# The block-doubling inverse of a gated DeltaNet layer on 32 by 32 and 64 by 64 tiles of TensorE's array

## What is computed

```python
a_low = jnp.where(strict, jnp.einsum('bhnid,bhnjd->bhnij', kb, k) * decay, 0.0)
t_mat = a_low + jnp.eye(C, dtype=a_low.dtype)
u = lax.linalg.triangular_solve(t_mat, vb, left_side=True, lower=True, unit_diagonal=True)
w = lax.linalg.triangular_solve(t_mat, kb * jnp.exp(gc)[..., None], left_side=True,
                                lower=True, unit_diagonal=True)
```

## Time and profile before

| | us |
|---|---|
| median of 3 runs (1456.88 to 1458.3) | 1457.95 |
| profiled execution, its own time | 1457.2 |
| span of that execution | 1455.2 |
| TensorE busy | 1433.1 (98%) |
| VectorE busy | 857.0 (59%) |
| ScalarE busy | 546.8 (38%) |
| POOL busy | 110.1 (8%) |

### The profile page before, as it was taken

The page is one execution under the profiler, slowest core; times in us unless marked ns, Lnnn a source line. Parts: engine busy times, 40 slices in busy tenths (PEclk is TensorE's granted clock), DMA queues, the critical chain, the costliest instruction groups (busy, mean ns, idle before and its releaser), DMA issues.

```text
span 1455.2 us, 28065 instructions
## 1 busy us (share of the span) xinstructions
PE 1433.1 (98%) x11980; PEld 1413.1 (97%) x11980; DVE 857.0 (59%) x1428; ACT 546.8 (38%) x1068; POOL 110.1 (8%) x149
## 2 busy tenths in 40 slices
PE   8999999999999999999999999999999999999997
PEld 8999999999999999999989999999999999999997
DVE  7746895778555554332486468958775555543334
ACT  5135563556222222222441364625562222222222
POOL 0001212100000100000000012221000000000000
PEclk9999999999999999999999999999999999999999
DMA  5332342122344333222213313411223433332221
GB/s 195 106 103 73 95 117 73 44 67 100 106 141 138 131 131 131 95 87 91 84 59 103 115 59 95 117 59 59 88 81 119 141 131 131 131 111 93 88 94 67
DMA packets 57692, 147.38 MB, mean 101 GB/s; under 512 B 19041, under 2 KB 22497, under 8 KB 57569
## 3 DMA queue, kind: packets, MB, share of 16 engines
q1 hardware_dynamic: 49744, 119.89, 25.3%
q0 software_dynamic: 7824, 25.70, 5.0%
HBM read 132.78 MB, written 12.78 MB: 100 GB/s over the span
## 4 chain that ended last, share of the span: by engine, by line
PE 89%; DVE 7%; ACT 2%; issue 1%; DMA 1%; SPq 0%; DVEq 0%; ACTq 0%
PE PS L566 73%; PE PS L572 4%; DVE Wl L1601 1%; DVE hT L1639 1%; PE PS L861 1%; PE PS L863 1%; DVE Xl L1618 1%; PE PS L844 1%; DVE mT L1638 1%; PE PS L755 1%; DVE conv L1726 1%; PE PS L1073 1%; PE PS L893 0%; PE PS L739 0%; PE PS L727 0%
## 5 line engine op out<-in xcount | busy, mean ns | idle before, releaser
L566 PE MATMUL PS<-Xh,Wh 128*128 128x260 f32 x2464 | 503.5, 285 | 3.3 <-DVE Xl L1660 2.7
L566 PE MATMUL PS<-Xl,Wh 128*128 128x260 f32 x2464 | 498.0, 283 | 0.0
L566 PE MATMUL PS<-Xh,Wl 128*128 128x260 f32 x2464 | 495.9, 283 | 0.0
L1141 ACT ACTIVATE Wh<-stage 128x1024 fp32r<-128x1024 f32 x211 | 223.6, 1060 | 654.7 <-PE PS L566 647.7
L566 PEld LDWEIGHTS PS<-Xh,Wh 128*128 128x128 f32 x2464 | 382.2, 189 | 6.7 <-DVE Xl L1660 3.1
L566 PEld LDWEIGHTS PS<-Xh,Wl 128*128 128x128 f32 x2464 | 379.9, 188 | 0.0
L566 PEld LDWEIGHTS PS<-Xl,Wh 128*128 128x128 f32 x2464 | 379.7, 189 | 0.0
L1601 DVE TENSOR_TENSOR Wl<-stage,Wh 128x1024 fp32r<-128x1024 f32 x211 | 258.0, 1223 | 183.5 <-ACT Wh L1141 183.0
L566 PE MATMUL PS<-actH,Wh 128*128 128x260 f32 x616 | 124.1, 283 | 0.0
L566 PE MATMUL PS<-actH,Wl 128*128 128x260 f32 x616 | 124.0, 282 | 0.0
L566 PE MATMUL PS<-actL,Wh 128*128 128x260 f32 x616 | 123.7, 282 | 0.0
(11 more groups left out here) (324 smaller groups left out, 1670.7 us busy)
## 6 DMA issues: line engine op xcount, KB each, us to landing
stage<-w_slabs SPq DMA_DIRECT2D x211, 512.0 KB, 3.3
dst<-state_ret POOLq DMA_DIRECT2D x32, 256.0 KB, 3.1
dst<-state_gdn POOLq DMA_DIRECT2D x32, 256.0 KB, 3.2
out_gdn_sample<-dst POOLq DMA_DIRECT2D x16, 256.0 KB, 2.8
out_ret_sample<-dst POOLq DMA_DIRECT2D x16, 256.0 KB, 3.1
hT<-x_t SPq DMA_DIRECT2D x3, 520.0 KB, 7.3
out_y_t<-hT SPq DMA_DIRECT2D x3, 520.0 KB, 3.0
hT<-x_t SPq DMA_DIRECT2D x2, 260.0 KB, 3.8
```

Source lines behind the costliest of these rows:

```text
L566: ins = mm(PS[:, 2 * slot + a, 0:HC], w[:, ws, pos, :], x[:, a, :], start=first and w is Wh and x is xh, stop=last and w is Wl)
L1141: A(Wh[:, G % NW], stage[:, G % NS], ACT.Copy).then_inc(s["hi_split"], 1)
```

## The change

The inverse is held in compact form (`Xc`): 64 columns for each matrix, its two halves of rows side by side in place of the zero blocks. All four chunks are one stage of each level, so there are three `left` and three `right`, one in each of the rounds 3 to 8, alternating. At the levels 16 and 32 each matmul is 32 by 32 by 64: four of them, on row groups 0 to 3 and column groups r (or r with the lowest bit turned), follow each other in the program. At the level 64 they are 64 by 64 by 64. At level 16 the weights are still masked by POOL (two calls); at the others the tile itself cuts out the block. `XT` is filled by two ScalarE copies (`inverse_rows`) and by the last VectorE step. `reads_back(1, B_U)` moves from the end of round 7 to behind the first block of round 8. VectorE takes its part of the inverse at t = 28 to 30 ahead of `lo`, and nothing of it stands behind the decode operations of t = 30 any more.

```diff
-        Yb = at("Yb", UP0, 0, [P, H, P])
...
-        XX_DIST = o + 3 * U - (2 * G_F + H * SEQ + 2 * NC * U)
-        XX = at("XX", A0, o + 3 * U - XX_DIST, [P, XX_DIST + NC * U])
-        Xinv = XX[:, 0:NC * U].rearrange("p (c h n) -> p c h n", c=NC, h=H)
-        XT = XX[:, XX_DIST:XX_DIST + NC * U].rearrange("p (c h n) -> p c h n", c=NC, h=H)
+        XT = at("XT", A0, o + 3 * U, [P, NC, H, P])
+        XC_AT = 2 * G_F + H * SEQ + 2 * NC * U
+        CX = H * NC * HB
+        Xc = at("Xc", A0, XC_AT, [P, 2, H, NC, HB])
+        Xinv = at("Xinv", A0, XC_AT, [P, NC, H, P])
...
+            return bass.AP(Xc, low + at_, [[2 * CX, P], [2 * b, n // (2 * b)], [up - low + b, 2], [1, b]])
...
                 def masked_step(i):
-                    n, k, c = l * STEPS + i, i // 2, 2 * (i % 2)
-                    if i < 2:
+                    if i == 0:
                         pool.wait_ge(s["mask_loaded"], 16)
                         pool.wait_ge(s["xq_stored"], (l + 1) * 32)
-                    else:
-
-                        pool.wait_ge(s["y_mm"], n - 1)
-                    mk = mask[:, k:k + 1, :].unsqueeze(1).to_broadcast([P, 2, 2, P])
-                    to = T[:, i % 2].rearrange("p (c a) n -> p c a n", c=2)
-                    nc.gpsimd.tensor_tensor(to, MT[:, c:c + 2, 2:4], mk, ALU.mult).then_inc(s["mtk_ready"], 1)
+                    mk = mask[:, 0:1, :].unsqueeze(1).to_broadcast([P, 2, 2, P])
+                    to = T[:, i].rearrange("p (c a) n -> p c a n", c=2)
+                    nc.gpsimd.tensor_tensor(to, MT[:, 2 * i:2 * i + 2, 2:4], mk, ALU.mult).then_inc(s["mtk_ready"], 1)
...
-                for u in range(10, 14):
+                for u in range(10, 16):
                     read_state(u)
-                masked_step(2)
-                for u in range(14, 16):
-                    read_state(u)
-                for i in range(3, STEPS):
-                    masked_step(i)
...
-                def left(i):
-                    m, b = l * STEPS + i, BL << i // 2
-                    pe.wait_ge(s["mtk_ready"], m + 1)
-                    if i == 0:
+                def left(k):
+                    b = BL << k
+                    if k == 0:
+                        pe.wait_ge(s["mtk_ready"], (l + 1) * 2)
                         pe.wait_ge(s["x_loaded"], (l + 1) * 2 * NBK * 16)
                         pe.wait_ge(s["bv_ready"], l * NC + 2)
                     else:
-                        pe.wait_ge(s["y_ready"], m)
-                    if i >= 2:
-                        pe.wait_ge(s["x_new"], m - 1)
-                    for j in range(4):
-                        ins = mm(PS[:, 4, j * P:(j + 1) * P], T[:, i % 2, j, :], firsts(2 * (i % 2) + j // 2, b, j % 2), start=True, stop=True)
+                        pe.wait_ge(s["x_new"], l * LEVELS + k)
+                    for p in range(2):
+                        for c in range(NC):
+                            to = slice((p * NC + c) * HB, (p * NC + c + 1) * HB)
+                            if k < 2:
+                                for r in range(4):
+                                    m = r if k == 0 else r ^ 1
+                                    w = T[rows_at(r, QB), c // 2, c % 2 * 2 + p, rows_at(m, QB)] if k == 0 else MT[rows_at(r, QB), c, 2 + p, rows_at(m, QB)]
+                                    ins = mm(PS[rows_at(m, QB), 4, to], w, first_of(b, p, c)[rows_at(r, QB)], start=True, stop=True)
+                            else:
+                                for g in range(2):
+                                    x = Xc[rows_at(g, HB), g, p if g else 2 + p, c, :]
+                                    ins = mm(PS[rows_at(1 - g, HB), 4, to], MT[rows_at(g, HB), c, 2 + p, rows_at(1 - g, HB)], x, start=True, stop=True)
                     ins.then_inc(s["y_mm"], 1)
 
-                def right(i):
-                    m = l * STEPS + i
-                    pe.wait_ge(s["y_ready"], m + 1)
-                    pe.wait_ge(s["second_ready"], m + 1)
-                    if i:
-
-                        pe.wait_ge(s["x_new"], m)
-                    else:
+                def right(k):
+                    b = BL << k
+                    pe.wait_ge(s["y_ready"], l * LEVELS + k + 1)
+                    if k == 0:
                         pe.wait_ge(s["bv_ready"], (l + 1) * NC)
-
-                    at_ = 0 if i // 2 < LEVELS - 1 else P // 2
-                    n = P - at_
-                    for c in range(2):
-                        for p in range(2):
-                            mm(PS[:, 5 + c, p * n:(p + 1) * n], sec[:, 2 * c + p, :], Y[i % 2][:, 2 * c + p, at_:P], start=True, stop=True)
-                        for p in range(2):
-                            ins = mm(PS[:, 5 + c, (2 + p) * n:(3 + p) * n], Y[i % 2][:, 2 * c + p, :], sec[:, 2 * c + p, at_:P], start=True, stop=True)
+                        pe.wait_ge(s["xt_ready"], l * 2 + 1)
+                    for p in range(2):
+                        for c in range(NC):
+                            to = slice((p * NC + c) * HB, (p * NC + c + 1) * HB)
+                            if k == 2:
+                                mm(PS[0:HB, 5, to], Xc[0:HB, 0, p, c, :], Y[0:HB, p, c, :], start=True, stop=True)
+                                ins = mm(PS[0:HB, 6, to], Y[HB:P, p, c, :], Xc[HB:P, 1, 2 + p, c, :], start=True, stop=True)
+                                continue
+                            for r in range(4):
+                                rows, own = rows_at(r, QB), rows_at(r % 2, QB)
+                                if k == 0:
+                                    w = sec[rows, (p * NC + c) * HB + r % 2 * QB:(p * NC + c) * HB + r % 2 * QB + QB]
+                                else:
+                                    w = Xc[rows, 1, 2 + p, c, own] if r % 2 else Xc[rows, 0, p, c, own]
+                                mm(PS[rows, 5, to], w, Y[rows, p, c, :], start=True, stop=True)
+                            for r in range(4):
+                                m = r if k == 0 else r ^ 1
+                                ins = mm(PS[rows_at(m, QB), 6, to], Y[rows_at(r, QB), p, c, rows_at(m % 2, QB)], second_of(b, p, c)[rows_at(r, QB)], start=True, stop=True)
                     ins.then_inc(s["x_mm"], 1)
 
-                def step_of_inverse(i):
-                    if i:
-                        right(i - 1)
-                    if i < STEPS:
-                        left(i)
-
                 def new_values(c):
 
                     if c == 0:
-                        pe.wait_ge(s["y_ready"], (l + 1) * STEPS)
-                        pe.wait_ge(s["x_new"], (l + 1) * STEPS - 1)
+                        pe.wait_ge(s["x_new"], (l + 1) * LEVELS)
+                        pe.wait_ge(s["xt_ready"], (l + 1) * 2)
                     else:
                         pe.wait_ge(s["t_ready"], l * (NC - 1) + c)
...
-                    proj(KT // 2)
+                    proj(1)
+                    if i == 8:
+                        reads_back(1, B_U)
+                    proj(KT // 2 - 1)
...
-                    elif i < 10:
-                        step_of_inverse(i - 3)
+                    elif i < 9:
+                        (right if i % 2 == 0 else left)((i - 3) // 2)
                     if i == 9:
 
                         new_values(0)
                         pe.wait_ge(s["dsq_ready"], l + 1)
                         mm(PS[:, 7, B_DN:B_DN + 2 * H * NB], ones, flat2(dn[:]), start=True, stop=True).then_inc(s["dsum_mm"], 1)
-                    if i == 7:
-                        reads_back(1, B_U)
...
-                def second_blocks(i):
-
-                    m, b = l * STEPS + i, BL << i // 2
-                    if i == 0:
-                        act.wait_ge(s["state_stored"], l * 32)
-                        act.wait_ge(s["x_loaded"], (l + 1) * 2 * NBK * 16)
-                    else:
-                        act.wait_ge(s["x_mm"], m)
-                    if i >= 2:
-                        act.wait_ge(s["x_new"], m - 1)
-                    for c in range(2):
-                        to = in_pairs(flat2(sec[:, 2 * c:2 * c + 2, :]), b)
-                        ins = A(to, seconds(2 * (i % 2) + c, b, 0, 2), ACT.Copy)
-                    ins.then_inc(s["second_ready"], 1)
+                def second_blocks():
+                    act.wait_ge(s["state_stored"], l * 32)
+                    act.wait_ge(s["x_loaded"], (l + 1) * 2 * NBK * 16)
+                    A(in_pairs(sec, BL), seconds(BL), ACT.Copy).then_inc(s["xt_ready"], 1)
+
+                def inverse_rows():
+                    act.wait_ge(s["x_new"], l * LEVELS + 2)
+                    act.wait_ge(s["x_zeroed"], (l + 1) * 2)
+                    for g in range(2):
+                        to = XT[rows_at(g, HB), :, :, rows_at(g, HB)].rearrange("p c h n -> p h c n")
+                        ins = A(to, Xc[rows_at(g, HB), 1], ACT.Copy)
+                    ins.then_inc(s["xt_ready"], 1)
...
```

(49 more changed lines are left out.)

56 lines of the change are left out of this document (29 added, 27 removed).

## The result

| | before | after |
|---|---|---|
| median (4 runs each) | 1457.41 us (1455.94 to 1458.3) | 1438.04 us (1436.87 to 1438.49) |
| profiled execution, its own time | 1457.2 | 1436.87 |
| span | 1455.2 | 1435.1 |

The ratio is 0.9866, with an interval from 0.9855 to 0.9878: 19.4 us less, between 17.8 and 21.1. The prediction was 16 us less, 1442.0.

The account below looks back on a forecast made before the run. PE, busy 98% of the span, was taken to bound the kernel. Tiles saving 13.3 us, plus 3.7 for a removed wait, less 1.0 for a new one, made 16.0 us less: 1442 us, range 1438 to 1453.

Parts of the forecast that it names:

- Item 2: The added 32 by 32 matmuls: 96 groups of four at 57 ns each, 5.5 us a layer.
- item 4: Changes of the array's tiling around the inverse's blocks in rounds 3 to 8: 1.8 us a layer, between 0.9 and 2.7.
- item 7: Other chains, from VectorE and ScalarE around the inverse's blocks, have cover; without it each would cost up to 1.5 us.
- Item 1: The old inverse's `left` and `right` matmuls removed, 144 passes: 15.77 us a layer.
- Item 3: The added 64 by 64 matmuls, 64 passes, two standing in the array at a time: 1.8 us a layer.
- item 5: `reads_back` moves and ScalarE's copy comes earlier, so PE's wait before the transpose goes: 3.7 us saved in two layers.
- item 6: VectorE's order at t = 30 adds a PE wait for `dsq_ready`: 1.0 us in all, between 0 and 1.6.
- A: Rival, chance 0.18: PE can't start small passes that fast, 28 ns a pass; only 5.6 us saved, 1452.3.
- B: Rival, chance 0.10: tiles on different row groups don't run together, 57 ns a pass; 16.7 us slower, 1474.7.
- C: Rival, chance 0.05: the clock falls to 1.2 GHz around rounds 3 to 8; 3 us more a layer, 1448.
- D: Rival, chance 0.07: tile arithmetic holds but a chain of item 7 is late, up to 1.5 us each; 1447 to 1450.

Follow-up runs that it names:

- the split block: Changed kernel with `right(0)` and `right(1)` each given in two halves, a projection block between them: 1438.97 us, ratio 0.9873 to the kernel before.

## Why the prediction was right in kind and 4.0 us short

The step that failed is the price of the tiles, items 2 to 4: 9.1 us a layer in the forecast, 8.2 in the traces. Item 2 took 57 ns for every group of four, which is too much for `right(1)`, and item 4's 1.8 us for the changes of tiling came out as 1.4. A second step is what item 7 and the list as a whole put at nothing: the time outside the stretches of the inverse fell too.

1442.0 less 1438.04 is 4.0 us. In parts: 0.5 is the kernel before, whose median is now 1457.41 and was 1457.95; 1.8 are the tiles; 1.6 lie outside the changed code.

*Item 1* is exact: the seven blocks are gone.

*Item 2* (5.5 us a layer). The price of a group of four, 57 ns, came out as 56, against bounds of 55 and 228. L755 was the right row to stand near: row groups add nothing. Where it failed is `right(1)`. The block takes 1.41 us where `right(0)`, with as many passes on four tiles in turn, takes 1.92: 11 ns a pass. The likely reason is that its two products use tiles (r, r) and (r, r with its lowest bit turned), eight different ones, so that no group of four has to wait for the one before it; the two blocks have their sizes and banks in common, but no run changed the tiles alone. So "a group can't beat its stream of 55 ns" holds between groups on the same four tiles and was no bound for the block. Without the last steps out, the 384 passes cost about 4.9 us: 0.6 a layer was too much.

*Item 3* (1.8): 32 steps of 58 ns, 1.87. In `right(2)` the two products of a pair have different row groups, write the same 64 partitions in two banks, and still run together.

*Item 4* (1.8) is the other term mis-sized. The stretch shrank by 8.92 us (the mean of the two layers); with item 5 adding 1.87 and item 6 taking 0.51, the new blocks and their changes of tiling cost 15.77 + 1.87 - 0.51 - 8.92 = 8.2 us. Less 4.9 and 1.9, that leaves 1.4: 0.13 us for the way out inside each of six blocks, 0.09 ahead of each of four (0.33 us from the last projection pair to the tiles instead of 0.24), and 0.3 in small pieces, most of it in the first projection matmuls behind the blocks, which start a little further apart. The step from the 20-column tiles to 32 by 32, for which I had taken 0.2, cost nothing more than the step to whole matmuls had: L791 to L849 is 0.33 us, L790 to L844 was too. The Trainium skill's "Changing tiling mode (not just tile) drains the TensorE" (TensorEngine Tiling, key properties) holds in kind; its price here is 0.22 us (0.09 in, 0.13 out) to 0.34 us (the split block) for a way in and out.

Together the tiles saved 7.6 us a layer where 6.7 was forecast, 1.8 us in two layers.

*Item 5* (3.7) is exact, and its cause is shown by two runs. *Item 6* (1.0): 0.51 twice; taking the wait away gave 0.7 a layer. *Item 7* held for the waits it names: no `left`, `right` or L889 waits.

So 1.6 us of the 19.4 isn't in the stretches that hold the changed code, where the traces show 17.8. The interval takes in 17.8 at its end. The start's clock comes and goes in both programs, but the time between the stretches does not quite: 681.7 to 682.8 us before, 680.3 to 680.4 in eight of ten profiles of the new inverse. "The DMAs of the blocks are as many as before and start no later: nothing" left out when they land: in layer 2 VectorE waited 1.3 to 2.9 us for `Aq` before and 0.7 to 1.5 after. How much of this belongs to the change, and by what way, stays open. I had put the range's lower end, 1438, at the small end of my own terms, and the time fell on that end, below the 1439 to 1446 that I had given the forecast itself.

*The rivals.* A: passes start 6 or 7 ns apart on different tiles and 14 or 11 ns on average; no floor of 28. The Trainium skill (TensorE: Matmul & The Clock Gate, "Wait — 56ns, not 53.3ns?") says that starts never come closer than about 25 ns, however few the columns. That doesn't hold between tiles; within one tile the trace shows 56 ns for 64 columns. B: the rule that row tiles can't access the same PSUM bank at the same time (the Trainium skill, TensorEngine Tiling, PSUM pressure) didn't bite where the four row groups go to four different column groups, as `left` has it. Whether it does for row groups on one column group and one bank, no run here tried. C: not in this kernel, but one order of the loops away. D: no chain that item 7 names was late.

## What to carry to other kernels

Where a block-diagonal product wastes the array, issue small tiles in rotation: a pass on each of four tiles costs what one pass costs (56 ns here), the block on eight distinct tiles took less still, and the same work tile by tile took three times as long, with the low clock behind it in the profile. Group tiled work, since each excursion from whole-array matmuls cost 0.22 to 0.34 us. Before moving an operation to get rid of a wait, look in the queue of the engine that feeds it: here the move alone gave four tenths of what the shorter queue gave. And take the same stretches in several profiles of both kernels before you call a difference elsewhere chance or gain: a difference of 1 to 2 us outside the change was partly the one and perhaps partly the other.

## What the hardware showed that was not expected

- The block on eight distinct tiles ran at 11 ns a pass (64 columns, float32), those on four in rotation at 14, and within one tile passes start 56 ns apart.
- 3.1 us of passes on one 32 by 32 tile after another were followed by 3.41 us at the lower clock level, in both layers of the profile; 1.0 us of the same passes in rotation were not in any profile.
- At the start of either program the granted clock may fall for 3.4 us, or not, in one execution or the next: 1.3 to 2 us.
- VectorE's copy of 24 columns took 1.3 to 1.8 us instead of 0.17 in each of the eight places where it met a MEMSET of POOL (1.81 us), and ended with it; PE stood for 1.1 to 1.2 us some 11 us later.
- Dense tile code stops now and then for up to 0.99 us without a wait, at places with one remainder by 256 in PE's instruction count. That the boundary between instruction packets has to do with it is likely; how is open, since no packet was under way during the stops.
